# The layer norms of a two-block transformer kernel in two halves of the tokens, with GpSimd making low parts

## Chip, cores and metric

The kernel runs on one core of a Trainium2 chip. The metric is the device time of one execution in microseconds (us), the median of several runs. TensorE is PE in the profile (PEld is its weight load), VectorE is DVE, ScalarE is ACT, GpSimd is POOL, SyncE is SP.

## What is computed

512 tokens of width 1024 go through a first block (gated convolution, dilated attention and two feed-forward parts) and then a second block of two layers. Only the second block's norms are touched. With h the tokens:

```python
for l in range(DEPTH):
    proj = h @ w_in[l]
    ...
    h = layer_norm_2(DEEPNORM_ALPHA * h + mixed @ w_out[l], ln1_g[l], ln1_b[l])
    ff = jnp.square(jax.nn.relu(h @ w_up[l])) @ w_down[l]
    h = layer_norm_2(DEEPNORM_ALPHA * h + ff, ln2_g[l], ln2_b[l])

def layer_norm_2(x, g, b):
    mu = jnp.mean(x, -1, keepdims=True)
    var = jnp.mean(jnp.square(x - mu), -1, keepdims=True)
    return (x - mu) * lax.rsqrt(var + LN_EPS) * g + b
```

## The kernel before

Activations lie with the features on the 128 partitions: X is 8 chunks (DC) of 128 features by 512 tokens (T), and every operation on a chunk is 512 columns wide. Each product of fp32 numbers is made of three matmuls of type fp32r: high weight by high data, high weight by low data, low weight by high data. So a chunk needs its high part HH (ScalarE, L936) and its low part HL (VectorE, L2212), and a weight slot needs the same.

Weights come as a stream of slots, 128 rows by 1024 columns each (512 KB). SP loads slot s into RAW[s % 2] when the low part of slot s - 2 is made; ScalarE makes the high part in WH[s % 2] (split_hi, L635), once TensorE is through with slot s - 2 (tile_done); VectorE makes the low part in WL[s % 2] (split_lo, L1832). A tile (project, L1211 to L1213) is one slot against all eight chunks of HH and HL: 24 matmuls of 512 columns into one PSUM bank.

A layer l of the second block is, in each engine's queue: mix_layer (22 tiles z0 + 0 to 21 with attention work between them, then the output projection: five slots by rows, add_rows at L1225 to L1227, and three slots by chunks, add_chunk at L1239 to L1241, 9 matmuls for each of 8 output chunks), layer_norm ln1, square_ffn (two halves of 16 up tiles and a down projection, 48 matmuls for each of 8 output chunks), layer_norm ln2. VectorE adds each finished output chunk to X (L1881, L1883; x_ready), and GpSimd folds X's chunks 0 to 6 into MU (fold_x, L572).

The norm itself: TensorE sums MU and X[7] over the partitions with a matrix of ones (sum_last, L1282 and L1284). VectorE takes the mean from the chunks (L2201, n_cent). ScalarE squares them (L640, n_sq), and TensorE sums the squares by quarters of the tokens, each quarter into 32 partitions (L1290). ScalarE takes the root (L652), VectorE the reciprocal (L1851), TensorE widens it back to all partitions (L1300, n_wide). Then, a chunk at a time, VectorE scales (L2208, n_row), ScalarE writes HH (L936) and the new X (L937, x_new), and VectorE writes HL (L2212). TensorE follows in first_tiles, which runs the first two tiles of the next projection chunk by chunk, the second four chunks behind the first (L1317, L1318, L1320). After the last norm SP stores X (L549).

At the start of mix_layer TensorE goes first_tiles, tile(2), gate_logits, swap(0), tile(3), tile(4), cumulate, tile(5), hidden. VectorE's queue there is lo(2), lo(3), lo(4), turn(0) (which waits for swap(0)), blocks(0), gate_logs, lo(5), blocks(1), lo(6), lo(s) being the low part of slot z0 + s. In square_ffn ScalarE's queue for each up tile is: ReLU of the tile from PSUM (L1185), the high part of the slot two further on, the high part of the squared result (L1188).

## Time and profile before

| | |
|---|---|
| median of 3 runs | 2451.67 us (2450.57 to 2452.4) |
| profiled execution | 2452.37 us, span 2450.6 us, mean granted clock 0.986 |
| TensorE matmul busy | 2362.8 us (96%) |
| VectorE, ScalarE, GpSimd busy | 57%, 44%, 7% |
| weight loads | 376 of 512 KB, 3.2 us each to landing |

Busy times are shares of the span. The ends of matmuls are modelled, so the step between two starts says more than a duration. An engine's idle time counts only where it stands in the chain that ends last.

### The profile page before, as it was taken

Reading aid. Unit: us, or ns where it says so; the run is one execution under the profiler, and the core shown is the slowest. Engines: PE = TensorE matmul, PEld = TensorE weight load, DVE = VectorE, ACT = ScalarE, POOL = GpSimd, SP = SyncE. Lnnn points to the kernel's source line nnn. Section 1 sums busy time; section 2 is a strip of 40 time slices with the busy share of each in tenths; the row PEclk is TensorE's granted clock in tenths of the full one; section 3 lists DMA queues with packets and bytes.
Section 4 is the critical chain, followed back from the end, with each engine's and each line's share of the span. In section 5 each row is a group of like instructions: output and inputs, shape, how many; then the busy total and the mean of one; then the engine's idle time right before and its main releaser. Section 6 shows DMA issues by size and latency. Waiting matters only on the chain.

```text
span 2450.6 us, 33040 instructions
## 1 busy us (share of the span) xinstructions
PE 2362.8 (96%) x11802; PEld 1908.6 (78%) x11802; DVE 1407.5 (57%) x2284; ACT 1086.7 (44%) x1687; POOL 169.0 (7%) x149
## 2 busy tenths in 40 slices
PE   8889999999999999999999989999989998999997
PEld 6667888887887888888777868888867776888886
DVE  6877777435775677742647764334354677532434
ACT  4554444326886444432437543223244663422322
POOL 0511000000000000000210010000013001000000
PEclk9999999999999999999999999999999999999999
DMA  4112222222121222222221112222222112222222
GB/s 172 61 58 89 100 97 94 94 102 79 52 77 52 98 99 94 94 99 100 90 71 43 52 69 94 96 101 95 95 92 83 36 44 78 86 94 95 102 96 78
DMA packets 57405, 208.32 MB, mean 85 GB/s; under 512 B 6478, under 2 KB 6880, under 8 KB 56928
## 3 DMA queue, kind: packets, MB, share of 16 engines
q1 hardware_dynamic: 56736, 204.51, 23.7%
q0 software_dynamic: 576, 2.52, 0.3%
q8 instruction: 65, 1.06, 0.2%
q14 instruction: 28, 0.23, 0.0%
HBM read 204.90 MB, written 2.10 MB: 84 GB/s over the span
## 4 chain that ended last, share of the span: by engine, by line
PE 71%; issue 18%; DVE 5%; ACT 2%; POOLq 2%; POOL 1%; DMA 0%; DVEq 0%; SPq 0%; ACTq 0%
PE PS L1211 13%; PE PS L1212 13%; PE PS L1213 13%; PE PS L1239 9%; PE PS L1240 9%; PE PS L1241 9%; DVE PS L1917 1%; ACT NB L640 1%; POOLq L607 1%; PE PS L1436 1%; DVE WL L1832 1%; PE PS L1424 1%; PE PS L1270 1%; POOLq L574 1%; PE PS L1320 1%
## 5 line engine op out<-in xcount | busy, mean ns | idle before, releaser
L1832 DVE TENSOR_TENSOR WL<-RAW,WH 128x1024 fp32r<-128x1024 f32 x376 | 481.3, 1280 | 426.9 <-ACT WH L635 425.6
L1211 PE MATMUL PS<-HH,WH 128*128 128x512 f32 x1792 | 707.4, 395 | 9.0 <-DVE KR L2114 4.5
L1213 PE MATMUL PS<-HH,WL 128*128 128x512 f32 x1792 | 698.7, 390 | 0.0
L1212 PE MATMUL PS<-HL,WH 128*128 128x512 f32 x1792 | 698.5, 390 | 0.0
L635 ACT ACTIVATE WH<-RAW 128x1024 fp32r<-128x1024 f32 x376 | 397.7, 1058 | 669.1 <-PE PS L1241 411.0
L1211 PEld LDWEIGHTS PS<-HH,WH 128*128 128x128 f32 x1792 | 337.1, 188 | 85.2 <-issue 6.8
L1212 PEld LDWEIGHTS PS<-HL,WH 128*128 128x128 f32 x1792 | 337.3, 188 | 71.1 <-issue 2.9
L1213 PEld LDWEIGHTS PS<-HH,WL 128*128 128x128 f32 x1792 | 336.9, 188 | 70.9
L1241 PE MATMUL PS<-MH,WL 128*128 128x512 f32 x864 | 336.1, 389 | 0.0
L1239 PE MATMUL PS<-MH,WH 128*128 128x512 f32 x864 | 336.1, 389 | 0.0
L1240 PE MATMUL PS<-ML,WH 128*128 128x512 f32 x864 | 336.1, 389 | 0.0
L1241 PEld LDWEIGHTS PS<-MH,WL 128*128 128x128 f32 x864 | 162.2, 188 | 33.8
L1239 PEld LDWEIGHTS PS<-MH,WH 128*128 128x128 f32 x864 | 162.2, 188 | 33.7
L1240 PEld LDWEIGHTS PS<-ML,WH 128*128 128x128 f32 x864 | 162.2, 188 | 33.5
L2494 DVE TENSOR_TENSOR SB<-RB 128x512 f32<-128x512 f32 x64 | 44.3, 692 | 166.9 <-ACT RB L1185 166.9
L2031 DVE SCALAR_TENSOR_TENSOR NBF<-NBF,VEC 128x511 f32<-128x511 f32 (+1 forms) x176 | 131.5, 747 | 14.1 <-issue 13.5
L1185 ACT ACTIVATE RB<-PS 128x512 f32<-128x512 f32 x64 | 38.3, 598 | 208.5 <-PE PS L1213 203.2
L2024 DVE TENSOR_TENSOR NBF<-PS,RSTD 128x512 f32<-128x512 f32 x88 | 60.8, 691 | 80.2 <-PE PS L1213 80.1
L834 ACT ACTIVATE PB<-PB,NEGMAX 128x512 f32<-128x512 f32 (+3 forms) x160 | 87.7, 551 | 22.2 <-DVE NEGMAX L2087 21.6
L2087 DVE CUSTOM_DVE_ANT_0 PB<-PS,TAB 128x512 f32<-128x512 f32 (+3 forms) x160 | 68.5, 486 | 26.5 <-issue 26.5
L1881 DVE TENSOR_TENSOR X<-X,PS 128x512 f32<-128x512 f32 x48 | 32.9, 685 | 88.4 <-PE PS L1241 88.3
L791 ACT ACTIVATE NBF<-NBF,VEC 128x512 f32<-128x512 f32 x88 | 70.4, 800 | 9.4 <-DVE NBF L2024 9.4
(300 smaller groups left out, 2552.3 us busy)
## 6 DMA issues: line engine op xcount, KB each, us to landing
RAW<-wstream SPq DMA_DIRECT2D x376, 512.0 KB, 3.2
X<-xt SPq DMA_DIRECT2D x4, 512.0 KB, 7.6
W<-cmp_w POOLq DMA_DIRECT2D x2, 1024.0 KB, 5.6
out<-X SPq DMA_DIRECT2D x8, 256.0 KB, 2.0
TAB<-tables SPq DMA_DIRECT2D x1, 1871.5 KB, 13.3
WS<-spatial_w SPq DMA_DIRECT2D x1, 512.0 KB, 8.8
BS<-spatial_b SPq DMA_DIRECT2D x1, 256.0 KB, 9.3
PW<-pool_w POOLq DMA_DIRECT2D x2, 128.0 KB, 2.3
```

What stands on the lines that cost most here:

```text
L635: act.activation(WH[:, b, :], RAW[:, b, :], ACT.Copy).then_inc(w_hi, 1)
L791: act.activation(ACCS[:, b, :], ZF[:, b, :], ACT.Identity, scale=w[:, 2:3], bias=w[:, 3:4]).then_inc(f_acc, 1)
L834: act.activation(row, row, ACT.Exp, scale=-1.0, bias=NEGMAX[:, 4 * e + i:4 * e + i + 1], accum_out=SUM[:, 4 * e + i:4 * e + i + 1]).then_i ...
L1211: pe.matmul(PS[:, bank, :], WH[:, b, w], HH[:, k, :], start=(k == 0), stop=False)
L1212: pe.matmul(PS[:, bank, :], WH[:, b, w], HL[:, k, :], start=False, stop=False)
L1213: last = pe.matmul(PS[:, bank, :], WL[:, b, w], HH[:, k, :], start=False, stop=(k == DC - 1))
L1239: pe.matmul(PS[:, bank, :], WH[:, b, w], rh, start=(rows + k == 0), stop=False)
L1240: pe.matmul(PS[:, bank, :], WH[:, b, w], rl, start=False, stop=False)
L1241: last = pe.matmul(PS[:, bank, :], WL[:, b, w], rh, start=False, stop=(k == count - 1))
L1832: dve.tensor_tensor(WL[:, b, :], RAW[:, b, :], WH[:, b, :].bitcast(F32), ALU.subtract).then_inc(w_lo, 1)
L2031: ins = dve.scalar_tensor_tensor(acc, ZF[:, b, 0:T - back], w[:, 2 - back:3 - back], acc, ALU.mult, ALU.add)
L2087: dve.tensor_tensor_reduce(PB[:, e, row], head_banks(e)[:, row], tab(mask)[:, T - w:T], 1.0, 3.0e38, ALU.add, ALU.min, NEGMAX[:, 4 * e + i ...
```

## The change

The four layer norms run in two halves of 256 tokens, h = 0 and h = 1.

- The last output chunks before a norm are made in halves (4 of 8 chunks before ln1, the last before ln2), half 0 of them first; add_rows does its matmuls for those chunks in halves too. Two halves share a PSUM bank.
- TensorE's order around a norm is in the new function seam. add_half, sum_half, squares_half and widen_half are the old steps on 256 columns (two of the four quarters). Each matmul still has a weight load of its own.
- Four tiles instead of two follow a norm in halves, in banks 0, 1, 4 and 5 (first_half): tiles 0 and 1 of half 0 with a lag of four chunks, then tiles 2 and 3 with none, then the same for half 1.
- Two more weight slots, WXH and WXL, hold the last two slots before a norm and the slots of tiles 2 and 3 behind it (parts, high_part, low_part).
- GpSimd makes HL of half 0 as X - HH, after ScalarE has written both (lows_half); VectorE makes that of half 1 as before.
- The root of a half is taken on 64 partitions, still over 128 columns, as is the reciprocal.
- After ln1 the ReLUs of tiles 0 to 3 are written out, and the high part of slot up + 4 stands behind the ReLU of tile 2. At the start of mix_layer tiles 2 and 3 come before gate_logits, and tile(4) and tile(5) before cumulate; VectorE's order is as before, but for lo(2) and lo(3) in layer 1.
- The load of W1 (1 MB) gets a semaphore of its own and is issued by GpSimd after tile 3. The stores are 16 of half the size.

```diff
--- before.py
+++ after.py
+FIRST_HALF = {f"mix{l}": 4 for l in range(DEPTH2)} | {f"down{l}1": DC - 1 for l in range(DEPTH2)}
+HALVES = (slice(0, TH), slice(TH, T))
+FIRST_BANKS = (0, 1, 4, 5)
...
+            def lows_half(fill, made):
+                for n in range(DC):
+                    pool.wait_ge(h_hi, fill + n + 1)
+                    pool.wait_ge(x_new, made + n + 1)
+                    cols = HALVES[0]
+                    pool.tensor_tensor(HL[:, n, cols], X[:, n, cols], HH[:, n, cols].bitcast(F32), ALU.subtract).then_inc(h_lo, 1)
...
-                fold_x(f"ln1_{l}")
-                fold_x(f"ln2_{l}")
+                fold_x(f"ln1_{l}", FIRST_HALF[f"mix{l}"])
+                lows_half(H_FILL[f"up{l}"], 2 * DC * 2 * l)
+                fold_x(f"ln2_{l}", FIRST_HALF[f"down{l}1"])
+                if l < DEPTH2 - 1:
+                    lows_half(H_FILL[f"in{l + 1}"], 2 * DC * (2 * l + 1))
...
-                squares(NB2, X, range(DC), n_cent, CENT[nm])
-                root(nm, 3, D)
                 bias = nm.replace("_", "_b")
-                for n in range(DC):
-                    act.wait_ge(n_row, ROWS[nm] + n + 1)
-                    if fill is not None:
-                        act.activation(HH[:, n, :], NB2[:, n, :], ACT.Identity, bias=vec(bias, n)).then_inc(h_hi, 1)
-                    act.activation(X[:, n, :], NB2[:, n, :], ACT.Identity, bias=vec(bias, n)).then_inc(x_new, 1)
+                for h, (cols, rows) in enumerate(zip(HALVES, HALF_ROWS)):
+                    for n in range(DC):
+                        act.wait_ge(n_cent, CENT[nm] + DC * h + n + 1)
+                        act.activation(NB2[:, n, cols], X[:, n, cols], ACT.Square).then_inc(n_sq, 1)
+                    act.wait_ge(n_sum, NORM[nm][1] + h + 1)
+                    act.activation(STD[rows, 0:P], PS[rows, SQUARE_BANKS[h], 0:P], ACT.Sqrt, scale=1.0 / D,
+                                   bias=tab("eps")[rows, 1:2]).then_inc(n_std, 1)
+                    if first is not None and h == 0:
+                        high_part(first + 2, first - 1)
+                        high_part(first + 3, first)
+                    for n in range(DC):
+                        act.wait_ge(n_row, ROWS[nm] + DC * h + n + 1)
+                        if fill is not None:
+                            act.activation(HH[:, n, cols], NB2[:, n, cols], ACT.Identity, bias=vec(bias, n)).then_inc(h_hi, 1)
+                        act.activation(X[:, n, cols], NB2[:, n, cols], ACT.Identity, bias=vec(bias, n)).then_inc(x_new, 1)
...
+                    for i in range(0 if half else 2):
+                        for b in range(2):
+                            act.wait_ge(tile_done, up + 2 * i + b + 1)
+                            act.activation(RB[:, b, :], PS[:, FIRST_BANKS[2 * i + b], :], ACT.Relu).then_inc(q_relu, 1)
+                            if i:
+                                split_hi(up // 2 + i, b + 2)
+                            act.wait_ge(q_sq, done + 2 * i + b + 1)
+                            act.activation(MH2[:, 2 * i + b, :], SB[:, b, :], ACT.Copy).then_inc(q_hi, 1)
...
+            def first_half(slot, fill, h, tiles):
+
+                cols = HALVES[h]
+                lag = 0 if tiles[0] else DC // 2
+                for b, k in [(b, step - b * lag) for step in range(DC + lag) for b in tiles]:
+                    if not 0 <= k < DC:
+                        continue
+                    if k == 0:
+                        pe.wait_ge(w_lo, slot + b + 1)
+                    wh, wl = parts(slot + b)
+                    w = slice(k * P, (k + 1) * P)
+                    bank = FIRST_BANKS[b]
+                    pe.wait_ge(h_hi, fill + DC * h + k + 1)
+                    pe.matmul(PS[:, bank, cols], wh[:, w], HH[:, k, cols], start=(k == 0), stop=False)
+                    pe.matmul(PS[:, bank, cols], wl[:, w], HH[:, k, cols], start=False, stop=False)
+                    pe.wait_ge(h_lo, fill + DC * h + k + 1)
+                    last = pe.matmul(PS[:, bank, cols], wh[:, w], HL[:, k, cols], start=False, stop=(k == DC - 1))
+                    if h and k == DC - 1:
+                        last.then_inc(tile_done, 1)
+
+            def seam(name, nm, high, low, fill, slot):
+
+                whole, count = FIRST_HALF[name], OUTS[name][2]
+                if whole == DC - 1:
+                    pe.wait_ge(x_ready, XR[nm] + DC - 3)
+                for n in range(whole, DC):
+                    add_half(name, n, 0, high, low)
+                if whole == DC - 1:
+                    add_half(name, whole, 1, high, low, range(0, 5))
+                    sum_half(nm, whole, 0)
+                    add_half(name, whole, 1, high, low, range(5, count - 2))
+                    squares_half(nm, 0)
+                    add_half(name, whole, 1, high, low, range(count - 2, count))
+                else:
+                    add_half(name, whole, 1, high, low)
+                    sum_half(nm, whole, 0)
+                    for n in range(whole + 1, DC - 1):
+                        add_half(name, n, 1, high, low)
+                    add_half(name, DC - 1, 1, high, low)
+                    squares_half(nm, 0)
+                widen_half(nm, 0)
+                if slot is not None:
+                    first_half(slot, fill, 0, (0, 1))
+                sum_half(nm, whole, 1)
+                if slot is not None:
+                    first_half(slot, fill, 0, (2, 3))
+                squares_half(nm, 1)
+                widen_half(nm, 1)
+                if slot is not None:
+                    first_half(slot, fill, 1, (0, 1))
+                    first_half(slot, fill, 1, (2, 3))
...
-                first_tiles(z0 // 2, H_FILL[f"in{l}"], 2)
-                tile(2)
+                if l == 0:
+                    first_tiles(z0 // 2, H_FILL["in0"], 2)
+                    project(0, z0 + 2, z_bank(2))
+                    project(0, z0 + 3, z_bank(3))
                 gate_logits()
                 swap(0)
-                tile(3)
                 tile(4)
+                tile(5)
                 cumulate()
-                tile(5)
                 hidden()
...
+                for n in range(whole, DC):
+                    add_half(name, n, 0, scale)
+                centre_half(0)
+                for n in range(whole, DC - 2):
+                    add_half(name, n, 1, scale)
+                invert_half(0)
+                for n in range(max(whole, DC - 2), DC):
+                    add_half(name, n, 1, scale)
+                scale_half(0)
+                if first is not None:
+                    low_part(first + 2)
+                    low_part(first + 3)
+                centre_half(1)
+                invert_half(1)
+                scale_half(1)
```

## Rows read from the trace of the kernel before

**Rows 1.** The page: busy times (share of the span) and instructions of each engine.
```profile
PE 2362.8 (96%) x11802; PEld 1908.6 (78%) x11802; DVE 1407.5 (57%) x2284; ACT 1086.7 (44%) x1687; POOL 169.0 (7%) x149
```

**Rows 2.** TensorE's waits, whole span: us in total, times, longest us.
```profile
PE PS L1300 <- DVE STD L1851: 14.9, 6, 6.3
```

**Rows 3.** The chain that ended last, in ln2_0: start us, us, what.
```profile
1801.17 0.86 PE PS L1282 x2
...
1808.70 0.47 PE PS L1290 x8
...
1809.59 0.96 DVE STD L1851
```

**Rows 4.** Timeline of ln2_0: start us, us, engine, line, operation, [idle before].
```profile
1800.77 0.40 PE L1241 MATMUL PS<-MH,WL 128*128 128x512 f32 x1
...
1803.11 4.87 DVE L2201 SCALAR_TENSOR_TENSOR X<-PS,X 128x512 f32<-128x512 f32 x8 [1.22 <-PE PS L1284]
...
1813.01 0.72 ACT L936 ACTIVATE HH<-NB,VEC 128x512 fp32r<-128x512 f32 x1 [3.45 <-DVE NB L2208]
1813.64 0.71 ACT L937 ACTIVATE X<-NB,VEC 128x512 f32<-128x512 f32 x1
...
1813.88 0.77 PE L1317 MATMUL PS<-HH,WH 128*128 128x512 f32 x1 [1.69 <-ACT HH L936]
...
1827.76 0.39 PE L1211 MATMUL PS<-HH,WH 128*128 128x512 f32 x1
```

**Rows 5.** The same of ln1_0, TensorE alone.
```profile
1436.36 1.12 PE L1282 MATMUL PS<-MU,TAB 128*128 128x512 f32 x2 [0.90 <-POOL MU L572]
...
1463.72 0.39 PE L1211 MATMUL PS<-HH,WH 128*128 128x512 f32 x1
```

**Rows 6.** Windows: us, busy of PE, PEld, DVE, ACT, POOL, granted clock, DMA, GB/s.
```profile
1442.52:1452.76 10.24, 6.91 (x43) 4.56 (x40) 7.23 (x11) 5.53 (x11) 0.00 (x0) 0.50 0.14 51
```

**Rows 7.** Groups by form, VectorE then ScalarE: count, busy us, mean ns.
```profile
L2087 DVE CUSTOM_DVE_ANT_0 PB<-PS,TAB 128x512 f32<-128x512 f32 x40 | 26.1, 686 | 26.5 <-issue 26.5
...
L2087 DVE CUSTOM_DVE_ANT_0 PB<-PS,TAB 128x256 f32<-128x256 f32 x40 | 15.4, 420 | 0.0
...
L1036 ACT ACTIVATE ZT<-PS 128x256 f32<-128x256 f32 x6 | 2.3, 384 | 8.7 <-PE PS L1601 8.7
```

**Rows 8.** GpSimd: its whole adds by form, then its timeline in the pooling.
```profile
L572 POOL TENSOR_TENSOR MU<-MU,X 128x512 f32<-128x512 f32 x20 | 25.8, 1289 | 105.0 <-DVE X L1881 95.9 <-DVE X L1883 8.2
...
1863.24 0.21 POOL L618 TENSOR_TENSOR PU<-PA,PU 64x16 f32<-64x16 f32 x1
1863.42 1.27 POOL L620 TENSOR_TENSOR PU<-PA,PU 64x496 f32<-64x496 f32 x1
```

**Rows 9.** Timeline, TensorE in unit_scores: eight matmuls; the last of them; its successor.
```profile
1304.01 1.55 PE L1622 MATMUL PS<-KB,ZS 128*128 128x512 f32 x8
...
1305.27 0.28 PE L1622 MATMUL PS<-KB,ZS 128*128 128x256 f32 x1
1305.39 0.39 PE L1211 MATMUL PS<-HH,WH 128*128 128x512 f32 x1
```

**Rows 10.** Timeline at the start of mix_layer(1): ScalarE, then VectorE.
```profile
1827.95 0.60 ACT L978 ACTIVATE ZT<-PS 128x512 f32<-128x512 f32 x1 [1.71 <-PE PS L1320]
...
1829.53 1.23 DVE L1832 TENSOR_TENSOR WL<-RAW,WH 128x1024 fp32r<-128x1024 f32 x1 [2.03 <-ACT WH L635]
```

**Rows 11.** The same a little later: TensorE, then VectorE.
```profile
1833.23 0.60 PE L1538 MATMUL PS<-TAB,ZT 128*128 128x128 f32 x4
...
1835.81 0.80 PE L1211 MATMUL PS<-HH,WH 128*128 128x512 f32 x1
...
1836.41 0.69 DVE L2259 TENSOR_TENSOR ZT<-ZT,TAB 128x512 f32<-128x512 f32 x1 [0.19 <-PE PS L1558]
...
1843.92 1.22 DVE L1832 TENSOR_TENSOR WL<-RAW,WH 128x1024 fp32r<-128x1024 f32 x1
```

**Rows 12.** Timeline at the end: ScalarE's last writes of X.
```profile
2442.89 5.33 ACT L937 ACTIVATE X<-NB,VEC 128x512 f32<-128x512 f32 x8 [3.02 <-DVE NB L2208]
```

More of the change, by code:

```diff
@@ L437, in program @@
         m_loaded = sem("m_loaded")
+        m_w1 = sem("m_w1")
         m_zero = sem("m_zero")
@@ L1247, in add_chunks @@
             def add_chunks(name, high, low, made, taken):
-                for n in range(DC):
+                for n in range(FIRST_HALF.get(name, DC)):
                     if n >= 4:
```

353 lines of the change are left out of this document (254 added, 99 removed).

## The prediction

> **What bounds the kernel now.** I read the page first: TensorE's matmuls cover 96% of a span of 2450.6 us [rows 1], in a run that took 2452.37. So only places where TensorE stands still or goes slowly are worth anything. The view of its waits puts the layer norms first: for a reciprocal (L1851) 14.9 us in 6 places, four of them the four norms [rows 2]. The chain of waits shows a norm as a ladder with no second lane: ones-sum, centring, squares, root, reciprocal, widening, scaling, high part, low part [rows 3]. TensorE's timeline gives its price in ln2_0: the last dense matmul starts at 1800.77, so the next could at 1801.00; the first new one starts at 1813.88; the two first tiles end where the third begins, 1827.76 [rows 4]. They hold 48 matmuls of 0.227 (the third tile's 24 take until 1833.23 [rows 11]), 10.9 us; of 26.75 us some 15.9 are lost. ln1_0 gives 27.4 - 10.9 = 16.5, with 0.9 of waiting for GpSimd's fold before [rows 5]; ln1_1 has the same pattern, 26.7 and the 0.9. The last norm takes from 2431.3 to the end, 19.3. All four: some 70 us, 2.8%. The granted clock is 0.50 (the 1.2 GHz level) for 7 to 10 us after the idle stretch of each of the four [rows 6], but there TensorE was waiting for its operands anyway.
>
> **The change: unit prices.** All whole-row work of a norm becomes halves of 256 columns. ScalarE: whole steps stand 0.63 apart in the fill (1813.01 to 1813.64 [rows 4]), 0.61 where nothing holds them; a read of 256 columns is busy for 384 ns [rows 7] against 0.60 for 512 [rows 10], 0.215 less, so a half costs 0.40, not 0.305. VectorE: eight centrings take 4.87, 0.60 each [rows 4]; L2087 takes 420 ns at 256 against 686 at 512 [rows 7], so a half centring costs 0.33, and a scaling or low part (0.66 whole) 0.39. Reciprocal (0.96 [rows 3]) and root keep their 128 columns and are paid twice. GpSimd: 16 columns take 0.21, 496 take 1.27 [rows 8]; 256 give 0.75. TensorE: after a matmul of 256 columns with its own 128-column weight load the next starts 0.12 later [rows 9]. I take 0.118 against half of 0.227, 9 ns for each matmul split. The bounds are 0 and 60 ns: the eight matmuls of that group hold 2560 columns, 1.135 by the column, and take 1.38 from 1304.01 to 1305.39 [rows 9], 0.03 more each. Over the 384 split matmuls outside the fills the upper bound is +20; the 0.12 is the nearer row, since it is of one 256-column matmul.
> The Trainium skill (VectorE: DVE Perf Modes, section "The TRN2 errata — SBUF-src ops pay a fixed extra latency per instruction") says that VectorE and ScalarE pay a fixed latency at each instruction, and advises tiles of at least 512 elements; its 224 + FD cycles at 1.2 GHz would be 0.613 and 0.400 us on ScalarE. The trace agrees, so by the page the sum would be the same; the rule speaks against halves.
>
> **ln1 (twice).** Zero is the end of chunk 3 of the output projection. TensorE does chunks 4 to 7 of half 0 by 4.25 (36 matmuls at 0.118) and one chunk of half 1 by 5.3. VectorE's last add ends at 5.2, GpSimd's fold of X6 at 5.8. The ones-sum (0.86, half of two such pairs [rows 3]) and 0.4 of handing over let centring start at 7.1. ScalarE squares from 7.6 to 10.7. TensorE comes from its other half chunks at 9.95 and needs 8 x 0.24 for the squares (a burst of four quarters is 0.47 now [rows 3]), to 11.9. From the last squares to the first tile's matmul it is 5.2 today (1808.70 to 1813.88 [rows 3, 4]); half a widening and half steps behind it leave 4.05, so 15.9. The high parts of tiles 2 and 3 fit on ScalarE under this.
> Fill of half 0: ScalarE writes HH and X in turn, 0.80 a chunk, GpSimd follows at 0.75, and sixteen matmuls (1.9) stand behind the last low part: 0.3 + 5.6 + 0.1 + 0.8 + 0.1 + 1.9 = 8.8, to 24.7, for 5.7 of matmuls. Only then comes the sum of half 1 in TensorE's queue, though its inputs are ready at about 14.5. Sum 0.86, tiles 2 and 3 of half 0 5.7, squares 1.9: 33.2; 4.05 again, with no cover: 37.2. Fill of half 1, 5.6 + 0.4 + 1.9 = 7.9: 45.1; tiles 2 and 3 of half 1, 5.7: 50.8. Today the stretch is 36 matmuls (8.2), 0.9, 27.4 or 26.7, and 48 matmuls (10.9): 47.4 and 46.7. That is +3.8 each. The five row chunks before it have 60 matmuls split: +0.5.
> Then something that the norm's own code doesn't show: tiles 2 and 3 end together, but ScalarE makes the high part of slot up+4 only after tile 2's ReLU, and VectorE's low part follows. Today the two tiles end half a tile apart and a whole tile covers this. From ScalarE's read of a tile to the end of such a low part it is 2.8 (1827.95 to 1830.76 [rows 10]); less 0.1, TensorE stands for 2.7 before the fifth tile. ln1: 3.8 + 0.5 + 2.7 = 7.0, twice: 14.0.
>
> **ln2_0.** Only chunk 7 is split, and more stands behind the chain. Zero is the end of its half 0: sum done 2.6, squares on ScalarE to 6.6, on TensorE to 7.8, first matmul 11.75, fill to 20.6, second chain (0.86 + 5.7 + 1.9 + 4.05) to 33.1, fill to 41.0, tiles to 46.7. Today: 5.45 + 26.75 + 10.9 = 43.1. With 0.2 for the split: +3.8.
>
> **The start of mix_layer.** The gate logits and the swap now stand after tile 3, with tiles 4 and 5 behind. VectorE runs turn, blocks, gate_logs and only then the low part of tile 5: from 1836.41 to 1845.14, 8.7 [rows 11]. Today tiles 3 and 4 cover it; then only tile 4 does, which starts 0.6 before the turn (1835.81) and takes 5.45. TensorE stands for 0.6 + 8.7 - 5.45 = 3.9 in layer 0. In layer 1 tile 4 also waits for its own low part, 2.8 less 2.6 of logits and swap (1833.23 to 1835.81), and the turn starts at once behind it: 3.7 in all.
> **The last norm.** Zero as in ln2_0. Scaling of half 0 from 10.6 to 13.4, ScalarE writes X to 14.3 and squares half 1 to 17.4; X of half 1 follows from 20.9 to 24.1. Today 5.45 + 16.9 (2431.3 to 2448.2 [rows 12]) = 22.35. With the split: +1.9. The stores' tail stays near 2.4.
> At nothing: W1's transfer behind tile 3 (hidden() wants it 15 us later), SP's waits (they change in count alone), and the small loads behind lows_half in GpSimd's queue (25 us ahead of use).
> **Sum:** 14.0 + 3.8 + 3.9 + 3.7 + 1.9 = 27.3. 2452.4 + 27.3 = 2479.7; the median is 0.7 below the profiled run, so 2479.
>
> **Rivals.** A, slower still (0.27), by any of three. GpSimd's half costs nearly a whole one, 1.29 [rows 8]: a fill is 8 x 0.54 = 4.3 longer, three times, +13, 2492. Or the clock is at 1.2 GHz in each fill: twenty half matmuls at 0.21 (half a column's time doubled) take 4.3, in which ScalarE's 0.80 for six would have supplied thirty-two; the twelve left are 1.4, six times: +8, 2488. Or VectorE and GpSimd block each other: two low parts of 1.23 [rows 11] fall into lows_half, 2.5 a seam, +7, 2487.
> On this the Trainium skill (SBUF — State Buffer, "The single rule" and what follows from it) says that a VectorE instruction with two SBUF inputs contends with a GpSimd one that reads SBUF, as a low part and a subtraction are; by it the time would be the last of the three. No row here isolates it.
> B, cost goes with columns (0.14). Halves at 0.305 on ScalarE and 0.30 on VectorE: fills of 7.7 and 7.1 and a chain shorter by 0.3, 2.5 a seam, -7.5: 2472. Rows 7 speak against it.
> C, faster (0.08), one mechanism: TensorE finds work through both chains and fills and never waits in a seam. Place: L1300 and L1317. Then ln1 is 8.5 + 1.7 + 3.9 + 1.3 + 22.7 = 38.1 instead of 47.1, ln2_0 35.3 instead of 43.1; with the gaps of the tiles still paid, 2 x (-9.0 + 3.2) - 3.9 + 3.9 = -11.6, 2441. It decides from the point where TensorE has more queued than the 4.05 from squares to matmul, and where a chunk's HH and X take under 0.71 (six matmuls). For it: half 1's chunks do stand under part of chain one. Against it: nothing stands under the last 4 us of either.
> D, no difference (0.06). The change doesn't hold back what I read it to: the low parts before tiles 4 and 5 are early (-13.0), and B (-7.5) and a shorter tail hold too: 2457.
>
> **How the numbers follow.** Forecast 0.45, A 0.27, B 0.14, C 0.08, D 0.06. The range takes in A's and B's ends and stops at 2461 and 2494; C, and the matmuls' upper bound (2499), are left outside. 0.2% (4.9 us) is about what can be told from no change here. Slower 0.86, same 0.06, faster 0.08.
>
> **What would show it.** TensorE's waits: the widening and the first matmul each wait 1 to 2 us, now twice a norm; a gap of 2.7 before the fifth up tile with ScalarE's read and high part in it; 3 to 4 us before tile 5 of each mix_layer, ended by WL; ScalarE's halves 0.40 apart; GpSimd's low parts near 0.75. The forecast is wrong if a seam of ln1 is under 47 us, if one of those gaps isn't there, or if 256-column matmuls step by much other than 0.118.

## The result

The changed kernel takes 2499.72 us (median of 4 runs, 2495.05 to 2501.51) against 2451.89 for the kernel before (4 runs): a ratio of 1.0197, 95% interval 1.0182 to 1.0211. It is 48 us slower, where 27 were forecast. The direction held, the size did not: the time lies outside the range given. Its profiled execution has a span of 2499.5 us, 48.9 more. (Of all executions below, one of experiment 11's ten stands apart, at 6110 us; its median would be the same to 0.01 without it.)

The page of the changed kernel, busy times; they answer to [rows 1]:
```profile
PE 2394.6 (96%) x12394; PEld 1972.9 (79%) x12394; DVE 1417.8 (57%) x2362; ACT 1100.3 (44%) x1779; POOL 193.2 (8%) x179
```
TensorE's waits (us in total, times, longest), in answer to [rows 2]:
```profile
PE PS L1339 <- DVE WL L2056: 19.4, 8, 5.7
PE PS L1687 <- DVE STD L2448: 9.7, 8, 1.4
...
PE PS L1429 <- DVE STD L2080: 8.9, 2, 6.3
PE PS L1706 <- POOL HL L661: 8.0, 6, 2.0
PE PS L1703 <- ACT HH L1037: 7.2, 6, 1.2
```
The wait of 6.3 us in [rows 2] is not gone: it belongs to a norm ahead of the second block, at 118.0 us, and is there as before (L1429). Of the 14.9 us only 5.9 were the four norms' (1.5 each); their eight halves now wait 9.7 (L1687). Two other waits have grown as well: for VectorE's low parts of weights (L1339) to 19.4, from 3.1 before, and for GpSimd's low parts (L1706) to 8.0, where VectorE's cost 1.4.

I cut both traces at the same matmuls (a stretch begins at the first matmul of its stage), so that every microsecond has a place:

| stretch | before | after | more | forecast |
|---|---|---|---|---|
| ln1_0, from the end of chunk 3 to the fifth up tile | 47.5 | 57.7 | 10.2 | 6.5 |
| ln1_1, the same | 46.8 | 56.6 | 9.9 | 6.5 |
| its fifth up tile | | | 1.8 | 0 |
| ln2_0, from chunk 7 to the end of four tiles | 48.5 | 55.7 | 7.2 | 3.8 |
| start of mix_layer(0), to the end of hidden() | 28.7 | 37.2 | 8.5 | 3.9 |
| start of mix_layer(1) | 17.8 | 26.6 | 8.8 | 3.7 |
| last norm | 30.2 | 33.0 | 2.9 | 1.9 |
| rest of the two mix_layers (split row chunks) | | | 1.5 | 1.0 |
| everything up to the first mix_layer | | | -1.9 | 0 |

(The "fifth up tile" is the first tile of the up projection behind the four that follow ln1. The fourth tile's 5.45, which the kernel before does behind the gate logits, counts with ln2_0 in both; mix_layer(0) begins at the end of its two first tiles. The -1.9 is scatter between executions and no effect of the change: in the experiments that point lies anywhere from 1192.3 to 1195.2.)

Every stretch that was forecast to grow grew, and most of them by about twice what was worked out. First what was sized rightly. Timeline of the changed kernel in ln1_0: TensorE's half matmuls, VectorE's half centrings, ScalarE's fill:
```profile
1433.90 0.28 PE L1657 MATMUL PS<-HH,WXH 128*128 128x256 f32 x1
1434.01 0.28 PE L1658 MATMUL PS<-HL,WXH 128*128 128x256 f32 x1
...
1441.22 2.74 DVE L2442 SCALAR_TENSOR_TENSOR X<-PS,X 128x256 f32<-128x256 f32 x8 [2.05 <-PE PS L1671]
...
1449.40 0.49 ACT L1038 ACTIVATE X<-NB,VEC 128x256 f32<-128x256 f32 x1
1449.80 0.49 ACT L1037 ACTIVATE HH<-NB,VEC 128x256 fp32r<-128x256 f32 x1
```
The half matmuls start 0.12 apart (0.120 over the 45 of this stage; 0.118 was taken, [rows 9]), a half centring takes 0.34, ScalarE's halves stand 0.40 apart, and the first tile's matmul comes 15.7 us behind the end of chunk 3 (15.9 worked out). The gap before the fifth up tile is there too, 2.7 long (2.54 in the row, which takes the end of the last matmul 0.16 late), and a low part of VectorE's ends it:
```profile
1491.57 0.50 PE L1339 MATMUL PS<-HH,WH 128*128 128x512 f32 x1 [2.54 <-DVE WL L2056]
```
Then where it went wrong. The fill of half 0 takes 12.4, 12.6 and 12.4 us in the three seams where 8.8 was worked out. Timeline of the changed kernel in ln2_0, GpSimd, VectorE, TensorE:
```profile
1824.95 7.95 POOL L661 TENSOR_TENSOR HL<-X,HH 128x256 fp32r<-128x256 f32 x8 [14.55 <-ACT X L1038]
...
1826.52 2.35 DVE L2061 TENSOR_TENSOR WXL<-RAW,WXH 128x1024 fp32r<-128x1024 f32 x2
...
1827.13 0.41 PE L1704 MATMUL PS<-HH,WL 128*128 128x256 f32 x1
1829.51 0.58 PE L1706 MATMUL PS<-HL,WH 128*128 128x256 f32 x1 [1.96 <-POOL HL L661]
```
VectorE makes its two low parts of weights from 1826.52 to 1828.87; the matmul that needs GpSimd's third low part stands until 1829.51, and none of GpSimd's arrives in between. The windows of the same kernel (us, busy of PE, PEld, DVE, ACT, POOL, granted clock, DMA, GB/s), the fill and the two tiles behind it:
```profile
1824.50:1837.20 12.70, 9.98 (x49) 9.42 (x50) 4.38 (x8) 5.89 (x15) 10.16 (x14) 0.60 0.30 99
1837.80:1843.90 6.10, 6.10 (x52) 5.94 (x52) 2.74 (x8) 2.74 (x8) 0.00 (x0) 1.00 0.00 0
```
The granted clock is 0.60 on average in the fill, the 1.2 GHz level for most of it, and full behind it.

At the start of mix_layer(0) the gap before tile 5 is 5.6 us, not 3.9 (the expectations below count it from the start of the last matmul and call it 5.9), and tile 5 itself takes 8.35 instead of 5.5. Timeline of the kernel before, VectorE's blocks(0) and blocks(1), then of the changed kernel, blocks(0) with GpSimd's sums and TensorE's wait for tile 5:
```profile
1206.49 4.36 DVE L2292 TENSOR_TENSOR TB<-ZT,CP 64x248 f32<-64x248 f32 x8 [0.16 <-issue]
...
1212.89 6.23 DVE L2292 TENSOR_TENSOR TB<-ZT,CP 64x248 f32<-64x248 f32 x8
```
```profile
1205.59 1.07 POOL L689 TENSOR_TENSOR PA<-PU 128x527 f32<-128x527 f32 x1
...
1209.98 6.43 DVE L2555 TENSOR_TENSOR TB<-ZT,CP 64x248 f32<-64x248 f32 x8 [0.16 <-issue]
...
1210.41 1.06 POOL L689 TENSOR_TENSOR PD<-PA 128x525 f32<-128x525 f32 x1 [3.75 <-issue]
...
1218.67 0.76 PE L1339 MATMUL PS<-HH,WH 128*128 128x512 f32 x1 [5.49 <-DVE WL L2056]
```
and its window over most of tile 5, columns as above:
```profile
1217.80:1224.60 6.80, 5.92 (x14) 4.69 (x15) 6.77 (x7) 0.00 (x0) 6.10 (x6) 0.50 0.24 77
```
The same eight instructions of blocks(0) take 6.4 instead of 4.4: the pooled tiles now come ahead of them, so GpSimd's window sums run beside them, where before they began behind them (1210.52). Behind the gap the granted clock is 0.50, the 1.2 GHz level, over most of tile 5.

### The profile page after: what moved, and what is told of

Read it like the earlier page. It is cut to its first block, busy times and chain, and to the rows that moved or that the text cites. A ratio compares the mean times of both kernels' runs of the same rounds, so it can differ in the third digit from the quotient of the medians.

```text
span 2499.5 us, 34398 instructions
## 1 busy us (share of the span) xinstructions
PE 2394.6 (96%) x12394; PEld 1972.9 (79%) x12394; DVE 1417.8 (57%) x2362; ACT 1100.3 (44%) x1779; POOL 193.2 (8%) x179
## 4 chain that ended last, share of the span: by engine, by line
PE 87%; DVE 7%; ACT 3%; DVEq 1%; POOL 1%; issue 1%; DMA 0%; SPq 0%; ACTq 0%; POOLq 0%
PE PS L1339 15%; PE PS L1340 15%; PE PS L1341 15%; PE PS L1375 9%; PE PS L1376 9%; PE PS L1377 9%; PE PS L1565 2%; PE PS L1553 1%; DVE WL L2056 1%; DVE PS L2153 1%; PE PS L1706 1%; PE PS L1703 1%; PE PS L1704 1%; PE PS L1844 1%; PE PS L1678 1%
## 5 line engine op out<-in xcount | busy, mean ns | idle before, releaser
L1339 PE MATMUL PS<-HH,WH 128*128 128x512 f32 x1744 | 693.2, 398 | 25.2 <-DVE WL L2056 19.4
L1340 PE MATMUL PS<-HL,WH 128*128 128x512 f32 x1744 | 684.4, 392 | 0.0
L1341 PE MATMUL PS<-HH,WL 128*128 128x512 f32 x1744 | 683.9, 392 | 0.0
L721 ACT ACTIVATE WH<-RAW 128x1024 fp32r<-128x1024 f32 x356 | 376.6, 1058 | 612.2 <-PE PS L1377 358.4
L2056 DVE TENSOR_TENSOR WL<-RAW,WH 128x1024 fp32r<-128x1024 f32 x302 | 377.7, 1251 | 275.5 <-ACT WH L721 274.1
L1339 PEld LDWEIGHTS PS<-HH,WH 128*128 128x128 f32 x1744 | 330.9, 190 | 101.9 <-issue 19.0
L1340 PEld LDWEIGHTS PS<-HL,WH 128*128 128x128 f32 x1744 | 330.8, 190 | 69.9 <-issue 2.6
L1341 PEld LDWEIGHTS PS<-HH,WL 128*128 128x128 f32 x1744 | 330.5, 190 | 69.9
L1375 PE MATMUL PS<-MH,WH 128*128 128x512 f32 x832 | 323.8, 389 | 0.0
L1377 PE MATMUL PS<-MH,WL 128*128 128x512 f32 x832 | 323.8, 389 | 0.0
L1376 PE MATMUL PS<-ML,WH 128*128 128x512 f32 x832 | 323.7, 389 | 0.0
L2061 DVE TENSOR_TENSOR WL<-RAW,WH 128x1024 fp32r<-128x1024 f32 x60 | 83.9, 1398 | 121.9 <-ACT WH L721 118.2
```

The source lines that it names most:

```text
L721: act.activation(WH[:, b, :], RAW[:, b, :], ACT.Copy).then_inc(w_hi, 1)
L1339: pe.matmul(PS[:, bank, :], WH[:, b, w], HH[:, k, :], start=(k == 0), stop=False)
L1340: pe.matmul(PS[:, bank, :], WH[:, b, w], HL[:, k, :], start=False, stop=False)
L1341: last = pe.matmul(PS[:, bank, :], WL[:, b, w], HH[:, k, :], start=False, stop=(k == DC - 1))
L1375: pe.matmul(PS[:, bank, :], wh[:, w], rh, start=(rows + k == 0), stop=False)
L1376: pe.matmul(PS[:, bank, :], wh[:, w], rl, start=False, stop=False)
```

## The experiments

Times are medians; the ratio is to the kernel before on the same chip, and its 95% interval follows in brackets. "Less" is counted from the 2499.7 of the changed kernel. That was measured beside a kernel before of 2451.9, the experiments beside one of 2449.9 to 2450.9, so these differences are up to 2.0 us too large, and an interval is worth some 4 us either way. Where a difference is under 5 us, the stretches of the trace show the effect and not the time alone.

**1. Low parts of weights behind the fill.**
```
             scale_half(0)
             if first is not None:
+                dve.wait_ge(h_lo, fill + DC)
                 low_part(first + 2)
```


> One wait is added to the changed kernel: VectorE's low parts of tiles 2 and 3 start only when GpSimd has made all eight low parts of half 0. Nothing is left out. In the changed kernel GpSimd's eight take 7.95 us in ln2_0 and the third one comes 2.4 late, while VectorE's two low parts run (1826.52 to 1828.87); the fill takes 12.6 against 8.8 worked out. If the lock-out alone makes the fill long, GpSimd's eight fall to 6.3 and the fill to 8.8, -3.7 in each of three seams, some -11 in all (2489). If the clock level (1.2 GHz from 1825.4 to 1835.6, a half matmul each 0.21) is what holds TensorE, the eight fall to 6.3 but the fill only to about 11.5, -1 in each seam, -3 in all (2497). If the low parts then come too late for tiles 2 and 3, a wait appears there and eats the gain.

2487.95, ratio 1.0152 (1.0136 to 1.0169): 11.8 less. GpSimd's eight low parts, then VectorE's two behind them:
```profile
1820.21 6.32 POOL L661 TENSOR_TENSOR HL<-X,HH 128x256 fp32r<-128x256 f32 x8 [14.81 <-ACT X L1038]
...
1826.57 2.36 DVE L2061 TENSOR_TENSOR WXL<-RAW,WXH 128x1024 fp32r<-128x1024 f32 x2 [4.70 <-POOL HL L661]
```
They take 6.3 instead of 7.95, 0.79 each (0.75 was taken), and the fills 9.4, 9.6 and 9.4: 3.0 less each, 9 of the 11.8 (9.8 against the kernel before of its own chip). That VectorE's low parts stop GpSimd is shown.

**2. No idle stretch for TensorE.**
```
+                    keep_busy(slot, 12)
                 widen_half(nm, 0)
+                keep_busy(slot, 10)
...
+                keep_busy(slot, 12, 3)
                 widen_half(nm, 1)
+                keep_busy(slot, 10)
...
                 tile(4)
+                kept(3)
+                for _ in range(24):
+                    pe.matmul(PS[:, 5, :], HH[:, 0, 0:P], HH[:, 0, :], start=True, stop=True)
                 tile(5)
```
(keep_busy makes that many matmuls of 256 columns whose results nobody reads; ahead of ln2_0's first widening it is 6.)


> Matmuls whose results nobody reads stand in TensorE's waits in the changed kernel: 12 of 256 columns between squares and widening and 10 between widening and first matmul of each half, and 24 of 512 columns (5.5 us) in the gap before tile 5 of both mix_layers. No wait and no other work changes. If the clock level costs time: granted clock 1.0 through the fills, half matmuls at 0.12, a fill of half 0 of about 10.4 instead of 12.4 (GpSimd's late third low part stays), tile 5 in 5.5 instead of 8.4 twice, and the first single tile of ln1_1 back by 1.7: some -14 in all (2485). If the fill is held by GpSimd alone: fills unchanged, only tile 5 gains, -6. If neither: the filler delays the chain, +1 to +3.

2494.81, 1.0181 (1.0164 to 1.0198): 4.9 less, 2.9 against the kernel before of its own chip, which the times alone do not tell from nothing. In the trace tile 5 runs at full clock and the starts of the mix_layers are 3.1 and 1.9 shorter; the fills of half 0 stay at 12.0 to 12.4, at a mean clock of 0.72 (0.59 and 0.60 without the added matmuls): TensorE still stands 2.4 in each for GpSimd. And the fifth up tile now runs slowly in both layers (7.2 and 7.1 us instead of 5.5), in the changed kernel in one.

**3. The edits of experiments 1 and 2 together.**
```
+                dve.wait_ge(h_lo, fill + DC)
...
+                keep_busy(slot, 12)
```


> The wait for GpSimd and the filler matmuls together, in the changed kernel. If both causes are there and each hides part of the other, the fill of half 0 comes to the 8.8 to 9 that was worked out: -3.6 in each of three seams, with tile 5 and the rest as with the filler alone, some -19 in all (2481), more than the two single gains added only if they overlap (3 + 14). If one of them isn't a cause, it equals the better of the two single runs.

2487.03, 1.0153 (1.0136 to 1.0170). Windows of this kernel, the fill of ln2_0 and the start of mix_layer(0):
```profile
1816.00:1826.00 10.00, 8.57 (x57) 7.34 (x57) 4.65 (x11) 7.26 (x17) 7.21 (x11) 1.00 0.02 3
```
```profile
1208.00:1225.00 17.00, 17.00 (x93) 14.25 (x93) 16.62 (x21) 6.52 (x9) 14.17 (x13) 1.00 0.12 42
```
With the stall and the low clock both gone the fills take 8.9, 8.8 and 8.8: the 8.8 that was worked out. So a fill's 3.6 too many were 3.0 of lock-out and 0.6 of clock. But the whole time is only 0.9 under experiment 1, which is within the scatter. In this kernel the 1.2 GHz stretch falls behind the gap before the fifth up tile, into dense work (1483.1 to 1486.5 and once more), where it costs half its length. That place is not chance alone: with the norms' waits filled (experiments 2, 3 and 13) the fifth up tile is slow in six of six cases, without, in three of the sixteen that have a gap before it. In the other thirteen such a stretch lies in a fill ahead of that gap, in eleven of them in the fill of half 1.

**4. VectorE makes the low parts of half 0.**
```
-                if n and h and fill is not None:
+                if n and fill is not None:
...
-                lows_half(H_FILL[f"up{l}"], 2 * DC * 2 * l)
```


> One part of the change is undone: VectorE makes the low parts of half 0 from NB2, as of half 1, and GpSimd makes none. If GpSimd is a worse place for them (it waits for X, takes 0.77 and is locked out), the first low part comes 0.7 sooner, no third one is late, and the fill of half 0 is clock-bound at about 11.3: -1.2 in each seam, 2496. If VectorE becomes the bound instead (a scaling and a low part, 0.75 a chunk, then two weight low parts of 1.2 before tile 2), a wait of about 1 us shows before tiles 2 and 3 of half 0 and the sum is 2499 or more.

2485.69, 1.0149 (1.0132 to 1.0166): 14.0 less (12.0 against the kernel before of its own chip), fills of 9.1, 8.0 and 9.0, which is 11.2 less in the three. The part of the change in GpSimd's hands costs more than it gives: 11 to 14 of the 48.

**5. GpSimd's window sums later.**
```
                 pool.dma_start(W1[:], cmp_w1[l]).then_inc(m_w1, 16)
+                pool.wait_ge(c_tb, 2 * l + 2)
```


> One edit: at the start of each mix_layer GpSimd starts its window sums only when VectorE's two stretches of blocks() are over. It tells apart why TensorE waits 5.9 and 6.1 us before tile 5, where 3.9 and 3.7 were worked out. Theory: VectorE's blocks() is slowed by the sums that GpSimd makes beside it (6.4 and 6.0 us in the changed kernel against 4.4 before); with the sums later blocks(0) takes 4.4 again and the gap falls to about 3.8 in both layers, so 4 us less in all, some 2496; the slow tile 5 behind the gap (8.4 instead of 5.6) stays, since it comes from the gap. Rival 1: blocks() is slow for a reason of VectorE's own (its place right behind turn, or what TensorE does): blocks(0) stays at 6 and the time at 2500. Rival 2: the sums are then late for their reader, and what is won at tile 5 comes back as a wait later in the layer: gap 3.8, time 2500.

2494.80, 1.0177 (1.0160 to 1.0194): 4.9 less (3.7 against its own kernel before). VectorE and GpSimd at the start of mix_layer(0):
```profile
1210.52 4.33 DVE L2556 TENSOR_TENSOR TB<-ZT,CP 64x248 f32<-64x248 f32 x8 [0.16 <-issue]
...
1216.89 4.29 DVE L2556 TENSOR_TENSOR TB<-ZT,CP 64x248 f32<-64x248 f32 x8
...
1221.26 2.10 POOL L690 TENSOR_TENSOR PA<-PU 128x527 f32<-128x527 f32 x1 [15.15 <-DVE TB L2556]
...
1217.12 0.76 PE L1340 MATMUL PS<-HH,WH 128*128 128x512 f32 x1 [3.39 <-DVE WL L2057]
```
Both stretches take 4.3 (6.4 and 8.3 beside GpSimd), and the gap before tile 5 is 3.5 in layer 0 and 3.9 in layer 1: the forecast's 3.9 and 3.7 were right for blocks() alone.

**6. The low part of tile 5 ahead of turn and blocks.**
```
                 lo(4)
+                lo(5)
                 turn(0)
                 blocks(0)
                 gate_logs()
-                lo(5)
```


> One edit: VectorE makes the low part of tile 5's weights ahead of turn(0), blocks(0) and gate_logs() instead of behind them. Theory: the gap before tile 5 (5.9 and 6.1 us) and the 1.2 GHz stretch that covers tile 5 (8.4 us where a tile takes 5.5) both come from that one place in VectorE's queue. Then tile 5 starts behind tile 4 in both layers and takes 5.5: 8.7 less each; VectorE's gate_logs() ends 1.2 later, and cumulate() behind tile 5 has to wait for it some 1 to 2 us: net 7 each, 14 in all, some 2486. Rival: the 1.2 GHz stretch has another cause (it belongs to tile 5's place, not to the gap): only the gaps go and tile 5 stays at 8.4, net 4 each, 2492. If it was all hidden anyway (cumulate() is held by gate_logs() and nothing before it matters) the gap moves from tile 5 to cumulate() and the time stays at 2500.

2500.07, 1.0204 (1.0187 to 1.0221): nothing. The theory fell. TensorE before hidden():
```profile
1226.13 2.15 PE L1787 MATMUL PS<-TB,W 128*64 128x62 f32 x35 [5.80 <-DVE TB L2555]
```
Tile 5 comes at once, and the gap stands two steps further on, 5.8 us in layer 0 and 6.3 in layer 1, at hidden(), which reads blocks(1); hidden() then takes 3.6 instead of 2.0, at a low clock as tile 5 did. The bound of this stretch is VectorE's whole queue up to blocks(1), not the one low part.

**7. Parts of slots up+4 and up+5 early.**
```
+                        if i == 0:
+                            high_part(up + 4, up + 1)
+                            high_part(up + 5, up + 2)
```
(behind the ReLU of tiles 0 and 1; VectorE's low parts likewise.)


> One edit in the first half of each ffn: ScalarE and VectorE make the high and low parts of weight slots up+4 and up+5 behind the ReLU of tiles 0 and 1 rather than behind that of tile 2. Theory: the 2.8 us that TensorE stands before the fifth up tile are the chain ReLU of tile 2, high part, low part, which nothing covers because tiles 2 and 3 end together; made early it goes, in both layers, and with it the 3.4 us at 1.2 GHz that follow (half of them lost, 1.7): 5.6 to 9, so 2491 to 2494. Rival: the fifth up tile waits for something else behind it (the bank that ReLU frees, or the next weights' arrival): the gap stays at 1.5 or more and the time is 2497 or above.

2491.32, 1.0168 (1.0151 to 1.0185): 8.4 less (7.2 against its own kernel before). The gap is gone in both layers, and the fifth up tile takes 5.5 in both. The gap's 2.7 was forecast; the 1.8 of clock behind it, in one layer, was not.

**8. Experiments 4, 6 and 7 together.**
```
-                lows_half(H_FILL[f"up{l}"], 2 * DC * 2 * l)
...
+                lo(5)
...
+                            high_part(up + 4, up + 1)
```


> Three edits at once: VectorE makes the low parts of the first half (measured alone: 14 us less than the changed kernel), the low part of tile 5 comes ahead of turn and blocks (14 expected), and the parts of slots up+4 and up+5 come early (6 to 9 expected). Theory: the three losses lie in different places and add up: 34 to 37 less, 2463 to 2466, and what is left over the kernel before, 13 to 16 us, is the bare price of halves (second chains that nothing covers, half steps that cost more than half). Rival: the places hide each other, because the stretch behind each has an engine that is late for its own reason (GpSimd's compressed sums, VectorE's gate logs): then the sum of the three alone is not reached and the time stays above 2472.

2480.42, 1.0119 (1.0102 to 1.0136). The time is the rival's, the reason is experiment 6's: its share is nothing, and 14.0 + 8.4 from 2499.7 is 2477.3. Two of the remaining 3.1 are the chips: with each difference taken against its own kernel before, 12.0 + 7.2 from 47.8 leaves 28.6, and 29.7 was measured.

**9. Tile 6 ahead of hidden().** On top of experiment 6:
```
                 cumulate()
-                hidden()
                 tile(6)
+                hidden()
```


> The run before this one moved the low part of tile 5 ahead of VectorE's turn and blocks, and the gap only moved: tile 5 came at once and TensorE then stood 6.1 and 6.6 us before hidden(), for VectorE's blocks(1); the time stayed at 2500. Theory: at the start of a mix_layer VectorE's own work (turn, two stretches of blocks, the gate logs, low parts) is the bound, and the changed order leaves one tile less of TensorE's work beside it than before. So, on top of that edit, tile 6 (5.5 us) is put between cumulate() and hidden(), as a tile stood there before, and its low part ahead of blocks(1). blocks(1) ends 1.2 later, TensorE comes 5.6 later: a gap of 1.5 to 2 is left, 4 to 5 less in each layer and no 1.2 GHz stretch worth more than 1: 9 to 12 less, 2488 to 2491. Rival: VectorE is late for tile 7's low part as well, so what is won at hidden() is lost again at tile 7: time 2496 or above.

2487.92, 1.0154 (1.0137 to 1.0171): 11.8 under the changed kernel, as expected (9.8 against its own kernel before). TensorE, layer 0:
```profile
1228.83 2.08 PE L1787 MATMUL PS<-TB,W 128*64 128x62 f32 x64 [1.45 <-DVE TB L2555]
```
The change had moved the gate logits one tile later and left one tile less of TensorE's work beside VectorE's queue; given back, 1.5 us of the gap are left in layer 0 and 2.3 in layer 1.

**10. The second chain earlier.** On top of experiment 4:
```
+                sum_half(nm, whole, 1)
                 if slot is not None:
                     first_half(slot, fill, 0, (0, 1))
-                sum_half(nm, whole, 1)
-                    first_half(slot, fill, 0, (2, 3))
+                    first_half(slot, fill, 0, (2,))
                 squares_half(nm, 1)
+                    first_half(slot, fill, 0, (3,))
```


> Two edits: VectorE makes the low parts of the first half (alone: 2485.7), and in TensorE's queue the ones-sum of the second half stands right behind the first widening and its squares between tile 2 and tile 3 of the first half. Theory: of the second chain, root, reciprocal, widening and first scaling (4.0 us in which TensorE waits) then lie under tile 3 (3.0 us); VectorE has centred and ScalarE squared the second half by the time tile 2 ends, so 2.9 less in each of the three norms that tiles follow: 2477. Rival: the second chain is held by ScalarE, whose queue has the fill of the first half (6.4 us) ahead of the squares of the second; then TensorE waits at the squares what it no longer waits at the widening, and the time stays above 2483.

2477.43, 1.0113 (1.0096 to 1.0130): 8.3 under experiment 4, where 2.9 in each of three norms was expected. The widening of half 1 waits for nothing now (1.45 before) in all three. The tail of the second chain without cover was real, and a matter of order.

**11. Experiments 4, 5, 7, 9 and 10 together.**
```
-                lows_half(H_FILL[f"up{l}"], 2 * DC * 2 * l)
...
+                pool.wait_ge(c_tb, 2 * l + 2)
...
+                            high_part(up + 4, up + 1)
...
                 tile(6)
+                hidden()
...
+                    first_half(slot, fill, 0, (3,))
```


> All repairs at once: VectorE makes the low parts of the first half, the parts of slots up+4 and up+5 early, the start of mix_layer with tile 6 before hidden(), GpSimd's window sums behind blocks(), and the second chain earlier in TensorE's queue. Theory (the losses lie in different places and are the ones named): from 2480.4 (three repairs) some 10 less at the two starts of mix_layer, 8.6 less for the second chains, 2 to 4 less from faster blocks: 2457 to 2460, still 6 to 9 above the kernel before, which is what halving costs in itself (reciprocal and root twice, half steps of 0.40 for 0.61 on ScalarE, half matmuls of 0.120 for 0.1135). Rival: the halves' ladder covers more than that once nothing is in its way, and the time comes under 2450; or the repairs collide in VectorE's queue and it stays above 2468.

2456.07, 1.0025 (1.0015 to 1.0035): 43.6 of the 48 are gone, or 41.6 of 47.8 against its own kernel before.

**12. Three tiles in one fill.** On top of experiment 11:
```
-                lag = 0 if tiles[0] else DC // 2
-                for b, k in [(b, step - b * lag) for step in range(DC + lag) for b in tiles]:
+                for b, k in [(b, step - b // 2 * (len(tiles) > 1)) for step in range(DC + 1) for b in tiles]:
...
-                    first_half(slot, fill, 1, (0, 1))
-                    first_half(slot, fill, 1, (2, 3))
+                    first_half(slot, fill, 1, (0, 1, 2))
+                    first_half(slot, fill, 1, (3,))
```


> On top of all repairs (2456), the order of TensorE's matmuls in the fills: tiles 0 and 1 side by side instead of half a tile apart, in the second half tile 2 with them, one chunk behind; VectorE centres the second half ahead of the low part of tile 3's slot, and ScalarE makes the high part of slot up+4 ahead of the first ReLU. Theory: what is left over the kernel before is TensorE starving in the fills, since ScalarE gives a chunk every 0.80 and two tiles take 0.72 of matmuls for it; with three, 1.08, it never waits, and the second fill with its tiles takes 11.8 instead of 14.4, in three seams; the first fill ends with 6 matmuls behind the last chunk instead of 16, 1.2 less, of which the second chain may take back up to all, as its squares are ready only about 11 us behind the start of the fill: 7.8 to 11 less, 2445 to 2448, which is at or just under the kernel before. Rival: what is left is the bare price of the halves on the path (two reciprocals, two roots, two widenings, matmuls of 0.120), and tiles 0 and 1, now done together and late, leave the ReLU and the parts of slot up+4 uncovered: a gap of 1.5 to 3 before the fifth up tile comes back and the time stays at 2453 or above.

2455.03, 1.0020 (1.0011 to 1.0029). 1.0 under experiment 11, or 2.0 with each against its own kernel before. Both mechanisms are there. The second fill with its tiles takes 11.9 in ln2_0 instead of 14.4, but in ln1 the rival's gap comes back. ScalarE, VectorE, TensorE in ln1_0:
```profile
1465.42 1.06 ACT L726 ACTIVATE WH<-RAW 128x1024 fp32r<-128x1024 f32 x1 [2.33 <-PE PS L1705]
...
1471.13 2.35 DVE L2064 TENSOR_TENSOR WL<-RAW,WH 128x1024 fp32r<-128x1024 f32 x2
...
1472.49 0.47 PE L1339 MATMUL PS<-HH,WH 128*128 128x512 f32 x1 [3.21 <-DVE WL L2064]
```
The high part is ready at 1466.5; the low part stands behind two squares of the ffn until 1471.1.

**13. The same with filled waits.**
```
+                keep_busy(slot, 12)
                 widen_half(nm, 0)
...
                 widen_half(nm, 1)
+                keep_busy(slot, 10)
```


> The kernel of the run before with matmuls that nobody reads (4 to 12 of 256 columns) in the places of both chains where TensorE waits. Theory: the granted clock still falls to 0.5 for some microseconds in each seam after the waits of the chains, and where three tiles are fed at once TensorE is not waiting for operands there, so it loses about half of that stretch: filled waits keep the full clock and give 1 to 1.7 us in each of three seams, 3 to 5 less than the run before. Rival: the fill is set by ScalarE's 0.80 a chunk all the same, the clock costs nothing, and the two times agree within 1.5 us, or the added matmuls delay the chain and the time is above.

2458.93, 1.0032 (1.0019 to 1.0044): 3.9 above experiment 12, with intervals that overlap; the traces agree with it. Windows of experiment 12 and of this one over ln1_0:
```profile
1438.00:1473.00 35.00, 30.21 (x238) 28.75 (x239) 24.16 (x51) 21.81 (x49) 0.72 (x1) 0.95 0.10 31
```
```profile
1438.00:1473.00 35.00, 31.14 (x257) 29.54 (x257) 23.69 (x50) 21.48 (x49) 0.68 (x1) 1.00 0.10 31
```
The clock is full in the seam (0.95 in experiment 12), and from the ones-sum to the fifth up tile it is no shorter, 42.65 against 42.2. As in experiment 3 the 1.2 GHz stretch then comes behind the gap, in the up projection (1473.4 to 1476.9). In experiment 12 the low clock lay in the fill of half 0, where it cost 0.7 (10.5 against 9.8 here); that is less than the 1.6 that it costs at the fifth up tile.

**14. Both ends.** On top of experiment 12: the low part of slot up+4 first in VectorE's ffn queue, and in the last norm the halves right behind each other:
```
                 centre_half(0)
+                if first is None:
+                    for n in range(whole, DC):
+                        add_half(name, n, 1, scale)
+                    centre_half(1)
+                    for h in range(2):
+                        invert_half(h)
+                        scale_half(h)
+                    return
```


> On top of the kernel with three tiles at once (2455.0, not the busy one): VectorE makes the low part of slot up+4 ahead of its first square of the ffn, and in the last norm, which no tile follows, the two halves go through the chain one right behind the other (ones-sum 1 behind the last add, centring 1 ahead of reciprocal 0, squares 1 and root 1 on ScalarE ahead of its writes of X) instead of one after the other. Theory: the gap before the fifth up tile (3.5 us, twice) was only VectorE's queue, which had two squares ahead of a low part whose high part was ready 4.6 us earlier; it goes to 0 to 0.5. And halves pay where they work as two stages of one ladder: from the end of half 0 of chunk 7 the last write of X comes some 18.7 us later, where one whole chain took 22.4 and the two chains of the changed kernel 24 to 25. Together 6 to 7 and 5 to 6 less: 2442 to 2444, under the kernel before by more than 0.2%. Rival: the low part of slot up+5, now the next in the queue, or the arrival of ScalarE's squares leaves the sixth tile or the down projection late by what the fifth gains, and in the last norm the reciprocals (0.9 each, whatever their rows) and VectorE's 6.4 us of scaling hold the end: under 4 us less in all, 2451 or above.

2444.82 against 2450.44, ratio 0.9977 (0.9968 to 0.9986): under the kernel before by 0.23%. The stretches of the table, this kernel against the one before: ln1_0 44.7 against 47.5, ln1_1 46.2 against 46.8, ln2_0 46.3 against 48.5, the last norm 30.6 against 30.2. Together that is 5.2 less, where the two profiled spans differ by 5.0, so the gain lies in the norms and the tiles behind them. ln1_1 gains less than ln1_0, since the clock falls in its second fill (13.3 us at 0.87, against 11.9 at 1.00). ScalarE at the end:
```profile
2430.65 0.36 ACT L1028 ACTIVATE STD<-PS,TAB 64x128 f32<-64x128 f32 x1 [3.85 <-PE PS L1691]
2430.92 2.54 ACT L1026 ACTIVATE NB<-X 128x256 f32<-128x256 f32 x8
...
2435.44 6.55 ACT L1033 ACTIVATE X<-NB,VEC 128x256 f32<-128x256 f32 x16
```
The last norm gave 2.9 from its ones-sum to the last write of X (22.3 to 19.4) and 2.1 as a whole (32.7 to 30.6), not 5 to 6: the squares of half 1 wait for the root of half 0, and all sixteen writes of X wait behind the second root. What none of these runs tells is how much of the gain is the halves and how much the four tiles behind a norm instead of two; a kernel with whole norms and four tiles was not run.

## Why the forecast was right in direction and wrong in size

**Unit prices: right.** 0.120 for 0.118, 0.40, 0.34 for 0.33, 0.79 for 0.75. Rival B (cost goes with columns) is out. Their sum was not measured by itself, but it cannot be most of the 48: experiment 14 keeps the halves everywhere and is under the kernel before. The opening reading of [rows 2] was wrong: it laid 14.9 us of waiting for a reciprocal to the norms, and 9.0 of them lie elsewhere. The sum does not use it.

**The chains of ln1 and ln2_0: right as far as they were worked out.** First matmul at 15.7 (15.9), gap before the fifth tile 2.7 (2.7), fills of 8.8 when undisturbed (8.8). The step that failed is the fill of half 0 in the changed kernel: the sum let GpSimd follow at 0.75 a chunk, while VectorE's two low parts stood in the same stretch. That was the third limb of rival A, priced at +7; it measured 3.0 a seam, 9, and it belonged in the sum. The Trainium skill (SBUF — State Buffer, "Who interferes with whom", with its "single rule") says that such a pair excludes each other, the second to issue blocked until the first has finished. The trace agrees: VectorE's two low parts end at 1828.87, and GpSimd's third is there at 1829.51. "No row here isolates it" was not so: in the trace of before VectorE's blocks(0) takes 4.36 with GpSimd idle and blocks(1), the same eight instructions, 6.23 beside its window sums. I had read the stretch [rows 11] only as a total.

**The start of mix_layer: the step that failed is "8.7 [rows 11]".** That length was carried over unchanged, though the change also moved GpSimd's sums to lie beside it: +2.1 in layer 0 and +1.9 in layer 1 (experiment 5). That the tile's wait was the only thing at stake was wrong as well: experiment 6 removed it and nothing was won, since hidden() waits for the same queue. The sign came out, and the 3.9 and 3.7 where GpSimd was held back (3.5 and 3.9); the reason behind them was half of the truth.

**The clock, "TensorE was waiting for its operands anyway": nearly right in a fill, wrong elsewhere.** It costs 0.6 in a fill of half 0 and up to 1.1 in one of half 1 (ln1_0, with its tiles: 14.9 us at a mean clock of 0.78, against 13.8 at full clock in experiments 2 and 3), but 2.8 at tile 5 in each layer and up to 1.8 at a fifth up tile, since there the stretch at 1.2 GHz covers dense work. The second limb of rival A put 8 us on the fills; most of what it cost lay outside them.

**Adding up:** the first fills 11.0 (9 of lock-out, 2 of clock), the second fills 1.7 (1.1 of clock), blocks() 4.0, tile 5 5.6, the fifth up tile 1.8, the last norm 1.0, together 25.1; less the 1.9 of scatter ahead of the change, 23, against the 21.6 that the forecast was short (48.9 - 27.3). VectorE and GpSimd in each other's way make 13 of it, the clock 10.5; the last norm's 1.0 I did not explain.

**Rivals C and D.** C's sum left out the last norm's +1.9. Its condition, that TensorE finds work through both chains and fills, was named rightly, and it is what experiments 10, 12 and 14 supply; the code as changed does not. D is out: no low part was early.

## To carry to other kernels

A step handed to an idle engine is not free if the two engines hold each other up, as VectorE and GpSimd did here (6.4 us for 4.4): look in the trace for the same instruction with and without that neighbour, before taking its price. When a reordering moves one wait, follow the late engine's queue to its next reader, since removing a wait alone often only moves it; what counts is how much other work lies beside that queue. And halving a chain pays only where the queues let one half's work run under the other half's waits; here the repairs, nearly all of them of order, took some 54 us off the change with every half kept.

## What the hardware showed beyond expectation

- Both sides of the pair lose: VectorE's eight instructions of 0.54 us take up to 8.3 together (4.3 alone), and GpSimd's sum at 1210.41 starts 3.75 us behind the one before it, where the same two stand 0.57 apart in the kernel before. VectorE's turn (1207.8 to 1209.8) lies in that time, but GpSimd was idle for 1.1 us ahead of it too, so that the whole wait comes from VectorE is not shown.
- Filling a wait with matmuls keeps the granted clock at 1.00 there, and the next unfilled wait is then the one behind which it falls to 0.50; in experiments 2, 3 and 13 that was the fifth up tile in both layers, where 3.4 us at half speed are 1.7 lost, and in a fill it had cost 0.6.
- The place of the fall also differs between seams of one kernel: in the changed kernel ln1_0 has it in the fill of half 1 (14.9 us, then a fifth up tile of 5.6), ln1_1 at the fifth up tile (13.8, then 7.2).
